# Pooling products in three fp32r passes, the last RG-LRU scan behind the second pooling mean, ScalarE's pooling squares ahead of the first gelu

## The reference

```python
n = rmsnorm(h, ln1_g)
proj = n @ w_in                                   # (1024, 1536): pool | lru | gate
# pooling: four groups of 128 columns, windows 2, 4, 8, 16
mean = (cs - lag) / minimum(pos, w)               # causal mean over w tokens
d = mean - u                                      # "the difference" of a group
y_pool = (d @ pool_w[g]) * pool_scale             # 128x128 matrix for each group
# recurrence: causal conv, two sigmoid gates, then
a = exp(log_a); b = sqrt(1 - a^2) * (i * xc); h_t = a_t * h_(t-1) + b_t
y_lru = h_t * gelu(u_gate)
mix = concat(rmsnorm(y_pool), rmsnorm(y_lru))
h = h + mix @ w_out
h = h + (silu(n2 @ w_gate) * (n2 @ w_up)) @ w_down; out = rmsnorm(h)
```

## Time and profile before

| what | value |
|---|---|
| median of 3 runs | 908.85 us (908.39 to 908.98) |
| the profiled execution | 908.8 us, span 906.9 us |
| mean granted TensorE clock | 0.998 |
| busy: PE, DVE, ACT, POOL | 891.6, 608.5, 389.9, 272.9 us |
| input projection with the mixers | about 11 to 171 us of the span |
| output projection | about 171 to 276 us |
| FFN | from there to 900 us |

### The profile page before, as it was taken

The page is one execution under the profiler, slowest core; times in us unless marked ns, Lnnn a source line. Parts: engine busy times, 40 slices in busy tenths (PEclk is TensorE's granted clock), DMA queues, the critical chain, the costliest instruction groups (busy, mean ns, idle before and its releaser), DMA issues.

```text
span 906.9 us, 10917 instructions
## 1 busy us (share of the span) xinstructions
PE 891.6 (98%) x3928; PEld 728.0 (80%) x3928; DVE 608.5 (67%) x852; ACT 389.9 (43%) x647; POOL 272.9 (30%) x211
## 2 busy tenths in 40 slices
PE   7999999999999999999999999999999999999996
PEld 6777777788888788888888888888888888888885
DVE  5678886664679856566565755556547976787666
ACT  6679424532565332233332333233334444445455
POOL 1000012543253745555545555555540000000000
PEclk9999999999999999999999999999999999999999
DMA  9011102114020223332233322333229933333324
GB/s 318 8 47 32 38 24 70 47 50 136 1 70 1 95 80 131 90 128 82 93 129 92 128 82 93 127 94 128 82 94 364 406 112 100 98 94 97 100 82 186
DMA packets 93678, 95.91 MB, mean 106 GB/s; under 512 B 5636, under 2 KB 63544, under 8 KB 93624
## 3 DMA queue, kind: packets, MB, share of 16 engines
q1 hardware_dynamic: 83240, 76.32, 24.9%
q10 hardware_dynamic: 10384, 18.88, 6.8%
HBM read 70.81 MB, written 24.38 MB: 105 GB/s over the span
## 4 chain that ended last, share of the span: by engine, by line
PE 95%; DVE 2%; ACT 1%; issue 1%; POOL 0%; DMA 0%; ACTq 0%; DVEq 0%
PE bank L1859 23%; PE bank L1860 23%; PE bank L1861 23%; PE bank L1750 4%; PE bank L1752 4%; PE bank L1751 4%; PE bank L1694 3%; PE bank L1696 3%; PE bank L1695 3%; PE bank L1769 2%; PE bank L1780 1%; PE bank L1728 1%; PE bank L1707 1%; DVE xc L1265 0%; DMA h<-in_x 0%
## 5 line engine op out<-in xcount | busy, mean ns | idle before, releaser
L662 POOL TENSOR_TENSOR r_lo<-gu_raw,r_hi 128x512 fp32r<-128x512 f32 x84 | 116.6, 1388 | 68.2 <-ACT r_hi L927 68.1
L662 POOL TENSOR_TENSOR r_lo<-wsum_S,r_hi 128x512 fp32r<-128x512 f32 x63 | 98.6, 1566 | 125.5 <-ACT r_hi L927 125.5
L1859 PE MATMUL bank<-T_hi,r_lo 128*128 128x512 f32 x336 | 130.9, 390 | 0.9 <-DVE u L1550 0.9
L1861 PE MATMUL bank<-T_hi,r_hi 128*128 128x512 f32 x336 | 130.7, 389 | 0.0
L1860 PE MATMUL bank<-T_lo,r_hi 128*128 128x512 f32 x336 | 130.7, 389 | 0.0
L1859 PE MATMUL bank<-d_hi,h_lo 128*128 128x512 f32 x308 | 119.8, 389 | 0.0
L1860 PE MATMUL bank<-d_lo,h_hi 128*128 128x512 f32 x308 | 119.8, 389 | 0.0
L1861 PE MATMUL bank<-d_hi,h_hi 128*128 128x512 f32 x308 | 119.8, 389 | 0.0
L927 ACT CAST r_hi<-gu_raw 128x512 fp32r<-128x512 f32 x84 | 52.2, 621 | 131.2 <-PE bank L1861 131.2
L1859 PE MATMUL bank<-nT_hi,r_lo 128*128 128x512 f32 x252 | 98.1, 389 | 0.0
L1861 PE MATMUL bank<-nT_hi,r_hi 128*128 128x512 f32 x252 | 98.0, 389 | 0.0
(11 more groups left out here) (218 smaller groups left out, 1622.6 us busy)
## 6 DMA issues: line engine op xcount, KB each, us to landing
h_raw<-hid_ops ACTq DMA_DIRECT2D x72, 256.0 KB, 2.6
gu_raw<-in_w_ffn_gate SPq DMA_DIRECT2D x22, 512.0 KB, 3.7
gu_raw<-in_w_ffn_up SPq DMA_DIRECT2D x22, 512.0 KB, 4.7
hid_ops<-hid SPq DMA_DIRECT2D x44, 256.0 KB, 2.3
dn<-in_w_ffn_down SPq DMA_DIRECT2D x44, 256.0 KB, 10.2
hid_ops<-hsum_S SPq DMA_DIRECT2D x33, 256.0 KB, 2.5
w_raw<-in_w_in SPq DMA_DIRECT2D x11, 512.0 KB, 3.8
h<-in_x SPq DMA_DIRECT2D x8, 512.0 KB, 6.7
```

Source lines behind the costliest of these rows:

```text
L662: pool.tensor_tensor(lo_of(n)[:], a_block(f, name), f32(hi_of(n)[:]), ALU.subtract)\
L1859: pe.matmul(bank, s_lo, m_hi, start=(opens and j == 0), stop=False, skip_group_check=True)
L1861: ins = pe.matmul(bank, s_hi, m_hi, start=False, stop=(closes and j == n - 1), skip_group_check=True)
```

## The change

The pooling products are made in three passes of fp32r, as the others are. So the pooling weights and the four differences get a high part (ACT: pool_weights_hi, pool_hi) and a low part (DVE: pool_weights_lo, pool_lo), in buffers of their own, and PE waits for the low parts. On DVE the last column of the recurrence is taken apart (gate_input, clamp, scan): the second pooling mean, column 7's low weights, first_half(6), a low part and pool_output(0) stand ahead of the last scan. The first addend of the squares goes to rg and the following ones to ig. ACT evacuates columns 4 to 7 with its waits at the second half, and in columns 8 and 9 takes the squares of a pooling group and (in column 8) the high part of the fourth difference ahead of the gelu of the first half.

```diff
--- before.py
+++ after.py
@@ -107,6 +107,11 @@
         y1_hi = at("y1_hi", 152.25, [P, GT, S], F32R)
         y1_lo = at("y1_lo", 168.25, [P, GT, S], F32R)
         sq_scr = at("sq_scr", 196.25, [P, 512])
+
+
+        pw_hi, pw_lo = at("pw_hi", 200.5, [P, GT, P], F32R), at("pw_lo", 188.25, [P, GT, P], F32R)
+        pd_hi = [at(f"pd_hi{p}", (164.25, 160.25, 164.25, 148.25)[p], [P, S], F32R) for p in range(GT)]
+        pd_lo = [at(f"pd_lo{s}", 120 + 4 * s, [P, S], F32R) for s in range(2)]
 
         xs2 = [at(f"xs2_{s}", 116 - 4 * s, [P, D]) for s in range(2)]
 
@@ -243,6 +248,7 @@
         sq_a_ok, sq_half_ok = sem("sq_a_ok"), sem("sq_half_ok")
         fin_act_ok = sem("fin_act_ok")
         psq_ok = sem("psq_ok")
+        pw_hi_ok, pw_lo_ok, pd_hi_ok, pd_lo_ok = (sem(n) for n in ("pw_hi_ok", "pw_lo_ok", "pd_hi_ok", "pd_lo_ok"))
         lsq_ok = sem("lsq_ok")
         ys_hi_ok, wo_hi_ok = sem("ys_hi_ok"), sem("wo_hi_ok")
         raw_ok = sem("raw_ok")
@@ -322,7 +328,8 @@
         def padded(i):
             return slice(PAD + i * HALF, PAD + (i + 1) * HALF)
 
-        ssum = [ig, ag]
+        ssum = [rg, ag]
+        ssq_next = ig
         wo_raw = w_raw[:].rearrange("p s k n -> p (s k n)").rearrange("p (k n) -> p k n", k=GT)
 
 
@@ -641,13 +648,13 @@
                     pool.wait_ge(psq_ok, 2 * p + 2)
                     if p >= 2:
                         pool.wait_ge(ssum_ok, p - 1)
-                    pool.tensor_tensor(ssum[0][:], ssum[0][:], rg[:], ALU.add).then_inc(ssum_ok, 1)
+                    pool.tensor_tensor(ssum[0][:], ssum[0][:], ssq_next[:], ALU.add).then_inc(ssum_ok, 1)
 
             def add_lru_squares(g):
                 pool.wait_ge(lsq_ok, g + 1)
                 if g >= 2:
                     pool.wait_ge(ssum_ok, GT - 1 + g - 1)
-                pool.tensor_tensor(ssum[1][:], ssum[1][:], rg[:], ALU.add).then_inc(ssum_ok, 1)
+                pool.tensor_tensor(ssum[1][:], ssum[1][:], ssq_next[:], ALU.add).then_inc(ssum_ok, 1)
 
             add_lru_squares(1)
             def nT_lo_a(m):
@@ -768,7 +775,7 @@
 
                 u = position(c, i)
                 act.wait_ge(proj_ok, u + 1)
-                if i == 0 and c >= 2:
+                if i == (1 if POOL0 <= c < GATE0 else 0) and c >= 2:
                     if c < POOL0 + 2:
                         act.wait_ge(xc_ok, c - 1)
                     elif c < GATE0 + 2:
@@ -792,8 +799,7 @@
                     act.activation(xc[c % 2][:, half(i)], src_, ACT.Identity,
                                    bias=v("conv_b", c), scale=v("conv_w", (TAPS - 1) * GT + c)).then_inc(u_ok, 1)
                 elif c < GATE0:
-                    if i == 1:
-                        act.copy(ub[c % 2][:, padded(i)], pj[u % 4][:]).then_inc(u_ok, 1)
+                    act.copy(ub[c % 2][:, padded(i)], pj[u % 4][:]).then_inc(u_ok, 1)
                 else:
                     src_ = ub[c % 2][:, padded(0)] if i == 0 else pj[u % 4][:]
                     act.activation(ub[c % 2][:, padded(i)], src_, ACT.Gelu_apprx_tanh).then_inc(u_ok, 1)
@@ -828,18 +834,31 @@
                     w = 2 * p + i
                     act.wait_ge(poolmm_ok, w + 1)
                     if w == 0:
+                        act.wait_ge(a_ok, GT)
+                    if w == 2:
                         act.wait_ge(scan_ok, GT)
                     if p >= 2 and i == 0:
                         act.wait_ge(ssum_ok, p - 1)
-                    dst = ssum[0] if p == 0 else rg
+                    dst = ssum[0] if p == 0 else ssq_next
                     act.activation(dst[:, half(i)], pg[w % 2][:], ACT.Square, scale=v("pool_scale", p))\
                         .then_inc(psq_ok, 1)
+
+            def pool_weights_hi():
+                act.wait_ge(small_in, 16 * 5)
+                act.wait_ge(rb_ok, 1)
+                act.copy(pw_hi[:], pool_ws[:]).then_inc(pw_hi_ok, 1)
+
+            def pool_hi(p):
+                act.wait_ge(d_ok, p + 1)
+                if p == 3:
+                    act.wait_ge(scan_ok, GT)
+                act.copy(pd_hi[p][:], xc[p % 2][:]).then_inc(pd_hi_ok, 1)
 
             def lru_squares(g):
                 act.wait_ge(lmul_ok, g + 1)
                 if g >= 1:
                     act.wait_ge(ssum_ok, GT - 1 + g - 1)
-                dst = ssum[1] if g == 0 else rg
+                dst = ssum[1] if g == 0 else ssq_next
                 act.activation(dst[:], y[1][:, g, :], ACT.Square).then_inc(lsq_ok, 1)
 
             def split_wo(q):
@@ -879,22 +898,39 @@
             split_w(3)
             sigmoids(0, 0)
             for c in range(2, NC_IN):
+                if c == POOL0 + 1:
+
+                    sigmoids(GT - 1, 0)
+                    split_w(c + 2)
+                    evacuate(c, 1)
+                    sigmoids(GT - 1, 1)
+                    pool_hi(0)
+                    decay(GT - 1)
+                    root(GT - 1)
+                    continue
                 if 1 <= c - 2 < GT:
                     sigmoids(c - 2, 0)
                 if 0 <= c - 2 < GT:
                     split_w(c + 2)
                     sigmoids(c - 2, 1)
                     decay(c - 2)
-                evacuate(c, 0)
+                if c < POOL0:
+                    evacuate(c, 0)
                 if 0 <= c - 2 < GT:
                     root(c - 2)
                 if 0 <= c - POOL0 - 2 < GT:
                     pool_squares(c - POOL0 - 2)
+                if 0 <= c - POOL0 - 1 < GT:
+                    pool_hi(c - POOL0 - 1)
+                if c >= GATE0:
+                    evacuate(c, 0)
                 if c == NC_IN - 1:
                     y_hi_part(0)
                     y_hi_part(1)
                     group_sqrt(0)
                 evacuate(c, 1)
+                if c == POOL0:
+                    pool_weights_hi()
                 if GT <= c - 2 < NC_IN - 4:
                     split_w(c + 2)
                 if c - 1 >= GATE0:
@@ -1269,13 +1305,15 @@
                         step(ins)
                 ins.then_inc(xc_ok, 1)
 
-            def recur(j):
-
+            def gate_input(j):
+                dve.wait_ge(gate_evac, 4 * j + 4)
+                dve.tensor_tensor(ig_ring[j % 2], ig_ring[j % 2], xc[j % 2][:], ALU.mult).then_inc(ix_ok, 1)
+
+            def clamp(j):
                 dve.wait_ge(t2_ok, j + 1)
                 dve.tensor_scalar(t2, t2, 0.0, None, ALU.max).then_inc(clamp_ok, 1)
-                dve.wait_ge(gate_evac, 4 * j + 4)
-                dve.tensor_tensor(ig_ring[j % 2], ig_ring[j % 2], xc[j % 2][:], ALU.mult).then_inc(ix_ok, 1)
-                split_w(j + 4)
+
+            def scan(j):
                 dve.wait_ge(sqrt_ok, j + 1)
                 dve.wait_ge(a_ok, j + 1)
                 step(dve.scalar_tensor_tensor(out=t2, in0=ag[:], scalar=1.0, in1=t2, op0=ALU.add, op1=ALU.mult))
@@ -1283,6 +1321,14 @@
                 b = ig_ring[j % 2]
                 step(dve.tensor_tensor(b, b, t2, ALU.mult))
                 dve.tensor_tensor_scan(y[1][:, j, :], ag[:], b, 0.0, ALU.mult, ALU.add).then_inc(scan_ok, 1)
+
+            def pool_weights_lo():
+                dve.wait_ge(pw_hi_ok, 1)
+                dve.tensor_tensor(pw_lo[:], pool_ws[:], f32(pw_hi[:]), ALU.subtract).then_inc(pw_lo_ok, 1)
+
+            def pool_lo(p):
+                dve.wait_ge(pd_hi_ok, p + 1)
+                dve.tensor_tensor(pd_lo[p % 2][:], xc[p % 2][:], f32(pd_hi[p][:]), ALU.subtract).then_inc(pd_lo_ok, 1)
 
             def window_mean(p):
 
@@ -1358,15 +1404,36 @@
                 rsqrt(gvar[:, t], gsd[:, t], grstd[:, t], tmp[:, 0:TT])
 
             for c in range(NC_IN):
-                if c >= 2:
+                if c == POOL0 + 1:
+
+                    first_half(c)
+                    pool_weights_lo()
+                    gate_input(GT - 1)
+                    pool_lo(0)
+                    clamp(GT - 1)
+                    window_mean(1)
+                    split_w(c + 2)
+                    first_half(c + 1)
+                    pool_lo(1)
+                    pool_output(0)
+                    scan(GT - 1)
+                    split_w(c + 3)
+                    continue
+                if c >= 2 and c != POOL0 + 2:
                     first_half(c)
                 if c == NC_IN - 2:
                     quadrant_matrices()
                     quadrant_sums(0)
                 if 0 <= c - 2 < GT:
-                    recur(c - 2)
-                if 0 <= c - POOL0 - 2 < GT:
-                    pool_output(c - POOL0 - 2)
+                    clamp(c - 2)
+                    gate_input(c - 2)
+                    split_w(c + 2)
+                    scan(c - 2)
+                if c > POOL0 + 2:
+                    if c - POOL0 - 2 < GT:
+                        pool_output(c - POOL0 - 2)
+                    if c - POOL0 - 1 < GT:
+                        pool_lo(c - POOL0 - 1)
                 if c < POOL0:
                     convolve(c)
                     if c == 0:
@@ -1382,7 +1449,7 @@
```

(9 more changed lines are left out.)

## The result

The changed kernel takes 910.21 us (median of 17 runs, 908.76 to 911.35), the kernel before 908.85 us beside it (908.21 to 909.21). The ratio is 1.0016, with a 95% interval of 1.0010 to 1.0023: slower by a sixth of a percent, inside the 0.2% that the prediction counted as the same, and inside its range of 907.4 to 910.6. But the 17 runs are not one heap. Eight lie from 908.76 to 909.89 us with a mean granted clock of 0.998 (one has 0.997), and nine from 910.21 to 911.35 us, all with 0.996; before, all 17 lie within 1.0 us. The lower group's middle is 909.6, the forecast was 909.5. What parts the two groups is rival B of the prediction, a fall of TensorE's clock, and several of the experiments are about that.

The account below looks back on a forecast made before the run. PE, busy 98% of the span, bounds the kernel. A 2.35 us stall for column 9's low weights, starting 1.00 us later, less 0.39 for the fourth pair, plus 0.11, nets +0.72: 908.8 becomes 909.5 us, range 907.4 to 910.6.

Parts of the forecast that it names:

- rival B: TensorE's clock falls in the 2.35 us stall ahead of column 9's first half unit: 5.45 us more, 914.9 us; chance 0.03.
- The PE term: Four pooling pairs on PE: three fp32r passes take 1.36 us against 1.75, 0.39 us less each, 1.56 for four.
- The 0.18 us stall at the second pair: PE's wait for a bank release; goes because pool_output(0) now stands ahead of the last scan on DVE, saving 0.18 us.
- The DVE sum: DVE's chain from 98.00 us without idle time: column 9's low weights ready at 132.61, 136.77 with POOL's adds.
- POOL's adds: Two POOL adds of squares meet busy DVE in window_mean(2) and window_mean(3), each costing DVE 2.08 us, 4.16 in all.
- Rivals A: A: POOL's adds cost DVE nothing, low weights ready at 132.7, PE never waits, 907.06 us; chance 0.06.
- A2: Only one of POOL's adds meets a held port: PE stalls 0.27 us at column 9's first half unit, 907.4 us; chance 0.08.
- 0.72 us: Net loss forecast on PE's path, from the stall ahead of column 9, the fourth pair's gain and a slower first matmul.
- Rival C: Pooling products on PE: fp32r costs as much as fp32, so the edit gains nothing there, 909.9 us; chance 0.04.

Follow-up runs that it names:

- The kernel with short adds: Changed kernel with POOL's first two adds of squares cut to 16 columns instead of 1024: 907.07 us.
- the longer one: Changed kernel with the subtract for column 9's low weights made twice, a stall of 3.45 us in its trace: 912.25 us.
- with the scan back: Changed kernel with the last scan ahead of the second pooling mean again: 913.52 us (4 runs).
- The second set: The changed kernel run again with no edit, 11 runs: 910.55 us.
- the fp32 experiment: Pooling products in fp32 again, on high parts alone, against the changed kernel with column 9's low weights ahead of window_mean(3) (907.07 us): 908.69 us.
- the third edit: ScalarE casts y 7's high part ahead of output weights, on top of column 9's low weights first and two reorderings (907.21, then 907.36 us): 905.85 us.

## Why the prediction was right, and where it was not

**The PE term** was right: 0.39 us for each pair was forecast, 0.40 measured with the products alone changed. The 0.18 us stall at the second pair is gone too (it starts at 115.39, with no gap).

**The DVE sum** was right. Low weights of column 9 were forecast to end at 136.77 and end at 136.74; the stall was forecast at 2.35 us and is 2.36, counted by starts as the prediction counts. No ScalarE, DMA or bank wait came in between, as argued.

**POOL's adds** were the step that decided the sign, and it held: both meetings took place, in window_mean(2) and window_mean(3), at 2.07 us each where 2.08 was taken. The kernel with short adds has no stall, so without these meetings the changed kernel would have none. Rivals A and A2 fall. The Trainium skill, "SBUF — State Buffer", section "SBUF: two separate sides", gives the lock; its "fully blocks" for the whole instruction would have meant 2.40. The traces agree on the blocking and put the loss at 2.07: POOL's first add ends at 121.00 and DVE's at 122.08, 1.08 us behind it and not a whole 1.23.

The second meeting rests on ScalarE's new order, the third part of the change. The first row below is ScalarE before, the second after:

```profile
137.80 1.25 ACT L835 ACTIVATE rg<-bank,vec 128x512 f32<-128x512 f32 x2
...
128.51 1.37 ACT L843 ACTIVATE ig<-bank,vec 128x512 f32<-128x512 f32 x2 [2.23 <-PE bank L1763]
```

Before, the third group's squares stood behind a gelu, and POOL's add came at 139.13, behind column 9's low weights; now it comes at 129.96, ahead of them. No run puts the old order back, so what this part of the change is worth by itself is not shown.

**The clock** was mis-judged, in its chance and in its price. The step that failed is the one in rival B: "The new stall of 2.35 us lies above the stretch that kept the clock, and no row says how the clock takes it", followed by a chance of 0.03 and a price of 5.45 us. The clock falls in 16 of 28 executions, by their times and mean clocks, and it costs 1.66 us in one trace and 1.51 in the longer one's. The price was wrong because it took a whole half unit at 1.2 GHz; in the trace the clock was back after 3.4 us, eight steps of 0.43 us instead of 0.23. The chance had no ground: between a stall that kept the clock (1.47 us) and an idle time that lost it, 2.35 us was an open question, and 0.03 claimed a knowledge that no row gave. The Trainium skill, "TensorE: Matmul & The Clock Gate", section "What's actually happening", says that an idle engine falls back to the slow clock. The traces agree for 3.45 us; for 2.20 us one trace of two does, at 0.57 from 138 to 142 us, and behind 2.28 us with the scan back the clock stayed at 1.00. So the rule was a second price on the stall, with a chance that these runs put near a half at this length.

With 0.72 us and half of 1.66 the forecast would have been 910.3. That the range of 907.4 to 910.6 held the median is partly luck: its upper end was set by other causes, and 910.21 is the lowest run of the upper group, which holds 9 of 17. The second set's median, 910.55, is just inside, and the middle of the upper group, 911.1, lies outside. The 909.5 was right for the executions that keep the clock, whose middle is 909.6.

**Rival C** fell with the fp32 experiment: fp32 cost 0.40 us more for each pair.

## What to carry to other kernels

Look for the row that has the least margin and nothing idle in front of it (here weights that were ready 0.63 us early), and put new work behind it; the same instructions gave 910.2 or 907.1 us by the place of one subtract. Work that is moved earlier on one engine moves its helpers too: POOL's adds came to stand beside a full DVE and cost it 4.1 us ahead of these weights, where they had cost 1.5. Where TensorE is the bound, a stall costs its length, and a longer one (here 2.20 us, not 1.4) can also cost the clock behind it, in some executions and not in others: read every run's time, not just the median and one trace.

## What was not expected of the hardware

- A stall of 2.20 us ahead of a matmul can cost 3.9: behind it the granted clock was 0.50 for 3.4 us, starting about 1 us into the resumed work, in one trace and not in the other, with the same 2.20 us in both. By times and mean clocks, stalls of 0.64 and 1.4 us at the same place never showed it in 22 runs, and one of 3.45 us did in all 5. A stall of 2.28 us at another place left the clock at 1.00 in its one trace.
- Taking away a wait of 1.5 us gave nothing twice, as another wait of 1.41 and then of 1.18 us took its place; the third edit gave 1.5 us at once, which is 1.2 us for the three together.
- An add of 16 columns on POOL still took 1.03 to 1.15 us, against 2.40 for 1024.
